# A streaming-encoder layer on one core: products that share one division of the TensorE array are put next to each other

## What is computed

```python
h = _rmsnorm(x, g)
(aq, ak, av, az, mq, mk, mv, mo, mz, mif, cb, cc, cx, cz, su, sz) = _split(h @ w_in)
...
s = jnp.einsum('bqhd,bkhd->bhqk', q, k_all).astype(jnp.float32) * (Dh ** -0.5)
p = jax.nn.softmax(s, axis=-1).astype(v_all.dtype)
o = jnp.einsum('bhqk,bkhd->bqhd', p, v_all).reshape(B, T, H * Dh)
...
_, _, x_re, x_im = lax.associative_scan(_ssm_combine, (a_re, a_im, bu_re, bu_im), axis=1)
y = (jnp.einsum('gcp,bsgp->bsgc', C_re, x_re) - jnp.einsum('gcp,bsgp->bsgc', C_im, x_im))
y = jax.nn.gelu(y)
...
x = x + (y @ w_out).astype(x.dtype)
```

## Time and profile before

| | |
|---|---|
| median of 3 runs | 2193.35 us (2192.39 to 2194.96) |
| the profiled execution's own time | 2191.37 us |
| its span, first to last instruction | 2189.7 us |
| PE busy | 99% of the span |
| mean granted TensorE clock | 0.999 of full speed |

### The profile page before, as it was taken

How to read it: one execution, slowest core, us unless ns; L and a number is a source line. 1 busy time by engine, 2 the same in 40 slices (tenths; PEclk the granted TensorE clock), 3 DMA queues, 4 the chain that set the end, 5 groups by cost and what they waited for, 6 DMA issues and landing times.

```text
span 2189.7 us, 32440 instructions
## 1 busy us (share of the span) xinstructions
PE 2166.2 (99%) x13058; PEld 2018.8 (92%) x13058; DVE 788.1 (36%) x1368; ACT 472.9 (22%) x803; POOL 408.1 (19%) x249
## 2 busy tenths in 40 slices
PE   8999999999999999999999999999999999999998
PEld 6999999999999999999999999999997997888887
DVE  7840222222213011127555322323311463353534
ACT  6510222121222111111111111111101033333432
POOL 0132222222222122223122222222221210000000
PEclk9999999999999999999999999999999999999999
DMA  9422415133242334332332333444453666564552
GB/s 370 142 81 84 166 38 191 56 108 127 90 154 85 111 147 147 145 104 75 95 88 67 86 111 114 131 133 137 147 161 120 222 204 216 185 247 160 198 197 96
DMA packets 179268, 303.07 MB, mean 138 GB/s; under 512 B 31836, under 2 KB 123996, under 8 KB 175600
## 3 DMA queue, kind: packets, MB, share of 16 engines
q1 hardware_dynamic: 171120, 285.62, 39.0%
q10 hardware_dynamic: 8064, 16.25, 2.2%
HBM read 243.24 MB, written 77.41 MB: 146 GB/s over the span
## 4 chain that ended last, share of the span: by engine, by line
PE 93%; DVE 3%; DMA 2%; ACT 1%; SPq 0%; issue 0%; DVEq 0%; POOLq 0%; ACTq 0%
PE G L990 22%; PE G L992 21%; PE G L991 21%; PE G L1351 3%; PE G L1353 3%; PE G L1352 3%; PE X L1353 2%; PE X L1351 2%; PE X L1352 2%; PE X L1128 1%; PE X L1328 1%; PE X L1088 1%; PE X L1119 1%; DMA orw<-w_out_t 1%; DMA x_lo<-x_t 1%; PE X L1222 1%
## 5 line engine op out<-in xcount | busy, mean ns | idle before, releaser
L990 PE MATMUL G<-hhi,whi 128*128 128x384 f32 x2832 | 963.4, 340 | 0.0
L992 PE MATMUL G<-hhi,wlo 128*128 128x384 f32 x2832 | 947.9, 335 | 0.0
L991 PE MATMUL G<-hlo,whi 128*128 128x384 f32 x2832 | 947.6, 335 | 0.0
L990 PEld LDWEIGHTS G<-hhi,whi 128*128 128x128 f32 x2832 | 531.9, 188 | 18.4 <-issue 9.3
L991 PEld LDWEIGHTS G<-hlo,whi 128*128 128x128 f32 x2832 | 532.2, 188 | 0.8
L992 PEld LDWEIGHTS G<-hhi,wlo 128*128 128x128 f32 x2832 | 531.8, 188 | 0.0
L964 POOL CAST whi<-wr 128x1024 fp32r<-128x1024 f32 x115 | 124.1, 1080 | 1345.6 <-PE G L992 1137.0
L966 POOL TENSOR_TENSOR wlo<-wr,whi 128x1024 fp32r<-128x1024 f32 x115 | 278.8, 2425 | 9.2
L1368 ACT ACTIVATE ev<-G 128x384 f32<-128x384 f32 x162 | 79.2, 489 | 712.0 <-PE G L992 700.6
L2172 DVE TENSOR_TENSOR olo<-orw,ohi 128x1024 fp32r<-128x1024 f32 x96 | 112.3, 1221 | 156.5 <-ACT ohi L1614 156.0
L1614 ACT ACTIVATE ohi<-orw 128x1024 fp32r<-128x1024 f32 x96 | 95.3, 1050 | 167.1 <-PE X L1353 60.1
(11 more groups left out here) (386 smaller groups left out, 1814.0 us busy)
## 6 DMA issues: line engine op xcount, KB each, us to landing
wr<-w_in_t SPq DMA_DIRECT2D x118, 512.0 KB, 5.4
orw<-w_out_t SPq DMA_DIRECT2D x96, 512.0 KB, 5.1
u_scratch<-ev SPq DMA_DIRECT2D x174, 192.0 KB, 1.9
x_lo<-x_t SPq DMA_DIRECT2D x7, 1536.0 KB, 13.4
xin<-x_all SPq DMA_DIRECT2D x9, 1024.0 KB, 13.7
yr<-y_scratch SPq DMA_DIRECT2D x12, 768.0 KB, 7.6
xo<-x_all SPq DMA_DIRECT2D x3, 3072.0 KB, 11.3
kT<-k_cache_t SPq DMA_DIRECT2D x8, 1024.0 KB, 7.4
```

The costliest lines, as they stand in the source:

```text
L990: mm(G[:, j, 0:GC], whi[:, kh, k], hhi[:, kk, hs], start=(kk == 0), stop=False)
L991: mm(G[:, j, 0:GC], whi[:, kh, k], hlo[:, kk, hs], start=False, stop=False)
L992: return mm(G[:, j, 0:GC], wlo[:, kh, k], hhi[:, kk, hs], start=False, stop=(kk == 15))
```

## The change

The products themselves stay the same. Moved or changed are:

- Streams: the new values of all 8 streams are turned at once after the attention (L1154 of the new file), copied back to `sv` by ACT, written to DRAM (`new_values`) and read back per stream into one of two `vnew` buffers. The values of stream b - 1 come directly before the scores of stream b, the turn of result b - 1 directly behind the turn of the probabilities of b. The values of stream 7 come behind the last segment, the turn of its result behind the first segment of S5.
- S5: `Vt` is turned where K was; K is made directly before the inputs. SP reads and writes the Toeplitz kernels two segments later. The results are made in the order st = 0, 2, 1, 3 in other places of the banks, with one count at the end instead of two.
- mLSTM streams: the products of division 128\*128 come ahead of the eight of 128\*32. GLU: the products of three row blocks stand together, then their segments.

```diff
@@ -623,7 +624,7 @@
 
             def load_keys(b, s):
                 sp.wait_ge(s_mm, 33)
-                sp.wait_ge(ss_mm, b)
+                sp.wait_ge(ss_mm, b + 1)
                 sp.dma_start(kT[s][:, :, :], k_cache_t[b]).then_inc(kc_in, 16)
 
             def attention(i, last):
@@ -662,11 +663,22 @@
...
             sp.dma_start(sbias[:, :], bias_s).then_inc(ab_in, 16)
...
+            sp.wait_ge(vt_ev, 1)
+            sp.dma_start(vN, sv[:, :, :].rearrange("p h n -> p (h n)")).then_inc(vn_in, 16)
+            sp.wait_ge(vn_in, 16)
+            load_new_values(0, 0)
+
             def streams(i, last):
                 for s in range(2):
                     b = 2 * i + s
                     sp.wait_ge(so_mm, 2 * b + 2)
                     sp.dma_start(vc[:, :, :], v_cache[b].rearrange("(t p) n -> p t n", p=128)).then_inc(vc_in, 16)
+                    if not (last and s == 1):
+                        sp.wait_ge(vn_in, 16 * b + 32)
+                        load_new_values(b + 1, 1 - s)
                     if not (last and s == 1):
                         load_keys(b + 1, 1 - s)
@@ -725,8 +737,9 @@
...
                 gemms(32 + 3 * f, 0, S5_CUTS[f], 3)
                 gemms(32 + 3 * f, 1, S5_CUTS[f], 3)
-                load_toeplitz(f)
                 for n, (t, kh, j) in enumerate(gemm_segs(2, S5_CUTS[f], 3)):
+                    if n == 2:
+                        load_toeplitz(f)
                     if n == 2 and not last:
                         sp.wait_ge(ab_done, f + 1)
                         load_bc(f + 1)
@@ -1135,59 +1148,81 @@
...
-
-
-            with pe.Fori(0, 4) as i:
+            pe.wait_ge(ss_in, 16)
+            pe.wait_ge(y_done, 33)
+            for hp in range(4):
+                last = tr(X[:, 4, 128 * hp:128 * hp + 128], sv[:, hp], ident[:, :])
+            last.then_inc(vt_mm, 1)
+
+
+            def stream_values(b, s):
+                pe.wait_ge(vc_in, 16 * b + 16)
+                pe.wait_ge(vt_ev, 1)
+                pe.wait_ge(vn_in, 16 * b + 32)
+                pe.wait_ge(pt_ev, 3 * b + 2)
...
+                last.then_inc(so_mm, 1)
+
+            def turn_result(b):
+                pe.wait_ge(pt_ev, 3 * b + 3)
+                tr(X[:, 0, 0:128], sO[:, :], ident[:, :]).then_inc(so_mm, 1)
+
+            def streams(i, first):
                 for s in range(2):
                     b = 2 * i + s
                     tg = list(gemm_segs(s, 2, 2))
-                    for t, kh, j in tg[:1]:
-                        gemm(24 + 2 * i + t, kh, j)
-                    pe.wait_ge(s_add, 33)
-                    pe.wait_ge(y_done, 33)
-                    pe.wait_ge(sy_done, b + 1)
-                    pe.wait_ge(kq_done, 4 * b + 1)
-                    for hp in range(4):
-                        last = tr(X[0:DT, 4, 128 * hp:128 * hp + 128], svb[:, hp], ident[:, :])
-                    last.then_inc(vt_mm, 1)
-                    for t, kh, j in tg[1:2]:
-                        gemm(24 + 2 * i + t, kh, j)
+                    if first and s == 0:
+                        gemm(24, tg[0][1], tg[0][2])
+                        pe.wait_ge(s_add, 33)
+                        pe.wait_ge(y_done, 33)
+                    else:
+                        stream_values(b - 1, 1 - s)
+                    if not first:
+                        pe.wait_ge(sy_done, b)
                     pe.wait_ge(kc_in, 16 * b + 16)
-                    pe.wait_ge(kq_done, 4 * b + 4)
+                    pe.wait_ge(kq_done, 3 * b + 3)
                     for hp in range(4):
                         mm(X2[32 * hp:32 * hp + 32, 0:512], qblk[:, hp], kT[s][:, hp, :], start=True, stop=True)
                     for hp in range(4):
                         last = mm(X2[32 * hp:32 * hp + 32, 512:SK], qblk[:, hp], skn[:, hp], start=True, stop=True)
                     last.then_inc(ss_mm, 1)
-                    for t, kh, j in tg[2:4]:
+                    for t, kh, j in tg[1 if first and s == 0 else 0:3]:
...
                     pe.wait_ge(ss_p, b + 1)
...
                     tr(X[0:DT, 3, 0:128], sS[:, 512:SK], ident[:, :]).then_inc(pt_mm, 1)
-                    pe.wait_ge(vc_in, 16 * b + 16)
-                    pe.wait_ge(vt_ev, b + 1)
-                    for t, kh, j in tg[4:5]:
+                    if not (first and s == 0):
+                        turn_result(b - 1)
+                    for t, kh, j in tg[3:6]:
                         gemm(24 + 2 * i + t, kh, j)
-                    pe.wait_ge(pt_ev, 3 * b + 2)
-                    for t in range(4):
-                        for hp in range(4):
-                            mm(X[32 * hp:32 * hp + 32, 4, 0:128], sPT[:, 128 * t + 32 * hp:128 * t + 32 * hp + 32],
-                               vc[:, t, 128 * hp:128 * hp + 128], start=(t == 0), stop=False)
-                    for hp in range(4):
-                        last = mm(X[32 * hp:32 * hp + 32, 4, 0:128], sPN[:, 32 * hp:32 * hp + 32],
-                                  vnew[:, 128 * hp:128 * hp + 128], start=False, stop=True)
-                    last.then_inc(so_mm, 1)
-                    for t, kh, j in tg[5:6]:
-                        gemm(24 + 2 * i + t, kh, j)
-                    pe.wait_ge(pt_ev, 3 * b + 3)
-                    tr(X[:, 2, 0:128], sO, ident[:, :]).then_inc(so_mm, 1)
...
+            streams(0, True)
+            with pe.Fori(1, 4) as i:
+                streams(i, False)
+            stream_values(7, 1)
...
             for f in range(4):
-                gemms(32 + 3 * f, 0, S5_CUTS[f], 3)
+                for n, (t, kh, j) in enumerate(gemm_segs(0, S5_CUTS[f], 3)):
+                    gemm(32 + 3 * f + t, kh, j)
+                    if f == 0 and n == 0:
+                        pe.wait_ge(sy_done, 8)
+                        turn_result(7)
                 pe.wait_ge(sy_done, 9)
                 pe.wait_ge(t1_done, 3 * f + 3)
+                pe.wait_ge(ab_done, f + 1)
+                for ri in range(2):
+                    for st in range(4):
+                        last = tr(X[:, ri, 128 * st:128 * st + 128], Vt[:, ri, st].rearrange("p t c -> p (t c)"), ident[:, :])
+                    last.then_inc(vt5_mm, 1)
+                gemms(32 + 3 * f, 1, S5_CUTS[f], 3)
                 pe.wait_ge(ca_done, f + 2)
@@ -1195,12 +1230,6 @@
                             last = mm(X[32 * st:32 * st + 32, 3 + a, 0:128], Bb[head_rows(a), ri, st],
                                       Wc[head_rows(a), ri, st, 0:LC].rearrange("p j c -> p (j c)"), start=(ri == 0), stop=(ri == 1))
                 last.then_inc(k5_mm, 1)
-                pe.wait_ge(ab_done, f + 1)
-                for ri in range(2):
-                    for st in range(4):
-                        last = tr(X[:, ri, 128 * st:128 * st + 128], Vt[:, ri, st].rearrange("p t c -> p (t c)"), ident[:, :])
-                    last.then_inc(vt5_mm, 1)
-                gemms(32 + 3 * f, 1, S5_CUTS[f], 3)
                 pe.wait_ge(vt5_ev, 2 * f + 2)
                 pe.wait_ge(u8_in, 128 * f + 128)
                 for ri in range(2):
@@ -1213,7 +1242,7 @@
...
                 pe.wait_ge(tz_in, 128 * f + 128)
-                for group in ((0, 1, 2), (3,)):
+                for group in ((0, 2), (1, 3)):
                     for st in group:
                         for a in range(2):
                             mm(output_place(st, a), Tz[:, 2 * st + a], u8[:, 2 * st + a], start=True, stop=False)
@@ -1221,7 +1250,7 @@
...
                                 last = mm(output_place(st, a), Wc[head_rows(a), ri, st, 1:LC + 1].rearrange("p j c -> p (j c)"),
                                           XS[head_rows(a), ri, st], start=False, stop=(ri == 1))
-                    last.then_inc(y5_mm, 1)
+                last.then_inc(y5_mm, 1)
                 gemms(32 + 3 * f, 3, S5_CUTS[f], 3)
@@ -1295,14 +1324,15 @@
...
-                for b in (0, 2, 4, 6, 1, 3, 5, 7):
-                    pair = slice(32 * (b // 2), 32 * (b // 2) + 32)
-                    mm(o[pair], qm[:, 128 * b + 32 * (b // 2):128 * b + 32 * (b // 2) + 32], ct8[h % 2][:, b], start=(b % 2 == 0), stop=False)
-                mm(o, WT[:, h], vn1[:, h], start=False, stop=True).then_inc(tp_done, 1)
                 pe.wait_ge(wkm_done, h + 1)
                 if h:
                     pe.wait_ge(n_done, h)
                 mm(X[:, 4, 0:NSTR], wsk[:, h], wsm[:, h], start=True, stop=True).then_inc(cn_mm, 1)
+                mm(o, WT[:, h], vn1[:, h], start=True, stop=False)
+                for b in (0, 2, 4, 6, 1, 3, 5, 7):
+                    pair = slice(32 * (b // 2), 32 * (b // 2) + 32)
+                    last = mm(o[pair], qm[:, 128 * b + 32 * (b // 2):128 * b + 32 * (b // 2) + 32], ct8[h % 2][:, b], start=False, stop=(b % 2 == 1))
+                last.then_inc(tp_done, 1)
                 for r in range(4):
@@ -1543,11 +1582,10 @@
...
-                act.wait_ge(y5_mm, 2 * f + 1)
+                act.wait_ge(y5_mm, f + 1)
```

(54 more changed lines are left out.)

32 lines of the change are left out of this document (22 added, 10 removed).

## The result

The changed kernel takes 2201.37 us, median of 7 runs (2199.07 to 2203.98); the kernel before, on the same chip, 2193.33 us (2191.90 to 2194.96). The ratio is 1.0039, 95% interval 1.0028 to 1.0049: slower by more than the 0.2% that can be told. The profiled execution took 2200.12 us with a span of 2198.4, 8.7 us more than the span of before.

The account below looks back on a forecast made before the run. PE, busy for 99% of the span, was taken to bound the kernel: 10.3 us more idle against 6.1 us less work gives +4.3, plus 1.2 for the clock, 2196.9 us, or 2198.9 us as a median; range 2194.8 to 2202.3 us.

Parts of the forecast that it names:

- the upper part of the range: A change of division priced between nothing and 0.35 us, so 15 are 0 to 5 us; range up to 2202.3 us.
- the forecast's own narrower range: Whole kernel, with at least one fall of the clock: 2198.0 to 2201.0 us, chance 0.45.
- What PE saves, 6.1 us: Streams, S5, mLSTM and GLU: fewer turns of values and fewer changes of division, at 0.2 us each, save 6.1 us.
- First scores, 4.9 us idle: First scores of the streams: PE arrives at 740.5, they start at 745.4, 4.9 us idle instead of 0.79.
- Rival 2: First scores: `sbias` lands 2 us earlier, so the wait is short; +2.3, 2195.7 us, chance 0.10.
- rival 5: A further wait, as for weights in the stream stage, paid by each stream; +8 or more, from 2201.5 us, chance 0.07.
- Vt of f = 0, 5.2 us idle: S5, turn of Vt at f = 0: starts 3.55 us later, at 1006.4; PE idles 5.2 us instead of 0.46.
- the 3.5 that the prediction gave as a sign: End of the streams: the last turned result should come 3.5 us later than 968.21.
- Rival 3: DVE's chain to Vt of f = 0 loses 4.75 us beside the weight splits; not slower, 2192.9 us, chance 0.09.
- Vt of f = 1, 2.3 us idle: S5, turn of Vt at f = 1: GELU ends 0.85 us later; PE waits 2.3 us instead of 0.85.
- The clock, +1.2 us: First scores and Vt of f = 0: even chance of a clock fall in each, 1.2 us per fall, one likeliest.
- the prediction's 6.7 us: Sum by the skill's HAM oscillation rule, where both long waits pay for the clock: 6.7 instead of 5.5 us slower.

Follow-up runs that it names:

- the rounds above: Changed kernel with two segments ahead of the first scores, last result in its old place, S5 results as Tz of two st then Wc of both: 2189.23 us, ratio 0.9981.
- the experiment: Changed kernel with the S5 result places, two counts and early GELU steps of before: 2200.50 us, ratio 1.0029 to the kernel before.
- the filled kernel: Changed kernel with unread products keeping PE busy in the waits at the first scores and Vt of f = 0 and 1: 2198.50 us, ratio 1.0022.

## Why the prediction was right, and which term was off

The forecast was slower by 5.5 us with a range of 2194.8 to 2202.3 us; it came 8.0 us slower (8.7 between the profiled spans), inside the range, and the waits and savings that it named are the ones that the trace has. But the clock cost 4.3 us more than it was given, and that the time still lies inside is in part luck: the upper part of the range was made for changes of division that cost nothing, and the forecast's own narrower range, with at least one fall, ended at 2201.0. By its steps:

- *What PE saves, 6.1 us.* Right in sum, 5.9. From one stream's scores to the next it is (941.71 - 772.21) / 6 = 28.25 us instead of 28.97 (774.47 to 803.44): 0.72 instead of the 0.65 us predicted, 5.0 us for seven, where 3.1 + 1.4 were counted. A head of the mLSTM stage's streams comes every 14.36 us (1574.53 to 1588.89) instead of 14.48 (1565.03 to 1579.51): 0.1, not 0.2 each, 0.4 instead of 0.8. K directly before the inputs gave 0.13 us per f, 0.5 in all (0.7 counted): from the first results of f = 1 to the first product behind the inputs of f = 2, past Vt, K and the inputs, it is 46.69 us (1130.40 to 1177.09) instead of 46.82 (1120.54 to 1167.36). The GLU gave nothing: six groups of 9.32 us and four of 11.90 hold the same 30.96 us besides their segments. The S5 results gave nothing: 5.41 us (1054.59 to 1060.00), before the same, about the 5.5 predicted. So one change of division is worth 0.12 (mLSTM) to 0.20 us (the rounds above), and at the streams 0.28 if the turn is taken at 0.44; the prediction's 0.2 for each is the right size and not one price. It also calls the transposes of the new values 128\*128, where their row prints 128\*16; they start 0.17 us behind a product like any other, so a smaller printed part alone doesn't cost.
- *First scores, 4.9 us idle.* It was 5.02, and they started at 745.52, predicted 745.4. Rival 2 did not come: DVE's wait for `sbias` ended at 744.86, before at 745.03. Nor did rival 5: the six distances from the second stream's scores to the last one's are 28.24 to 28.26 us.
- *Vt of f = 0, 5.2 us idle.* It was 4.05. PE came 2.45 us later than reckoned (1003.30 instead of 1000.85), which the 2.7 us of the fall at the scores explain, and the last turned result stands at 974.21, 6.0 us later than 968.21 and not the 3.5 that the prediction gave as a sign. Vt came only 1.3 us later (1007.69 instead of 1006.4): from the gate to `BC` took 6.86 us instead of 7.74 (968.61 to 976.35 before), and DVE's chain from `BC` to Vt 26.16 instead of 26.44. Timeline of DVE, the changed kernel:
```profile
974.52 0.22 DVE L1953 TENSOR_TENSOR sz<-X,sz 64x64 f32<-64x64 f32 x1 [17.87 <-PE X L1174]
...
981.38 0.20 DVE L1989 TENSOR_SCALAR BC<-BC 128x64 f32<-128x64 f32 x1 [5.50 <-DMA BC<-s_c]
...
990.65 2.45 DVE L2012 TENSOR_TENSOR E<-E,w 128x128 f32<-128x128 f32 x1
...
1006.85 0.69 DVE L2030 TENSOR_TENSOR Vt<-Vt,w 128x512 f32<-128x512 f32 x1
```
  The slowed steps are still there: L2012 took 2.45 us and L2011 ahead of it 1.04, where the same two lines took 0.29 and 2.37 before, and the four slowed steps hold 5.5 us more than like ones without a split beside them, before 5.7. Rival 3 did not come.
- *Vt of f = 1, 2.3 us idle.* It was 2.39, and the late GELU is 0.8 us of it, as the experiment showed. The three GELU steps took 1.26 us, as reckoned (1.3), although the row that the prediction names for it, 0.41 us for 288 columns, is 1.4 ns each; the 0.95 us for 864 are 1.1.
- *The clock, +1.2 us.* This is the step that was mis-sized. The prediction said "an even chance for each, so one fall is the likeliest: +1.2". It fell in both, and in the 2.39 us at f = 1, which the prediction did not count at all (the 2.41 us elsewhere, the nearest in length that it had, had held). And a fall did not cost 1.2 us but 1.4 at Vt and 2.7 at the scores: the 1.2 came from nine matmuls at the kernel's start, but behind these waits the transposes and five products, or the scores and twelve products, ran slowly. Read from rows 5.5 us, by the filled kernel 4 to 6.

As a sum: 9.4 us more idle (10.3 predicted) and 5.5 for the clock (1.2), less 5.9 saved (6.1), are 9.0 us; the spans differ by 8.7. The Trainium skill, "TensorE: Matmul & The Clock Gate", section HAM oscillation, says that gaps between bursts of matmuls put the engine back to its lower clock; the prediction's 6.7 us by it took both long waits but the price of one short burst. The trace agrees with the rule at these places (1.2 GHz behind all three), and its 8.7 us is 2 us above that sum; in the kernel with rounds 3.57 us of idle had no fall.

## What to carry to other kernels

Small products that share an array division belong next to each other, but the segment between them was also the cover of a wait: before it is moved, look at which load or which chain sets the next start, and leave that segment where it is. Price a wait of PE of over 2 us, which may bring a fall, with what runs behind it at the low clock, here 1.4 to 2.7 us on top of the wait itself, and if it can't be covered, put work into it that has to be done anyway (K), or even work that nobody reads. Serial chains that begin at the last small product (gate, stores, BC, Vt) start as late as that product does.
